# Half of the weighted one-hots of a route quad move from VectorE to ScalarE

## The chip, the cores and the metric

The kernel runs on one core of one Trainium2 chip. The time is the device time of one execution in microseconds; the median of several runs counts. A row of the trace gives a start on the clock of the one profiled execution, in microseconds from its first instruction.

## The reference, cut to what matters

Two layers of a streaming encoder. Each has a mixer of three attention branches, which the change does not touch, and then a PEER layer: for each of 512 tokens, product keys pick 16 of 128x128 experts for each of 8 heads, so 128 experts a token, each with a softmax share.

```python
def peer_ffn(h, w_q, sub_keys, u_tab, v_tab):
    ...
        q = (xb @ w_q).reshape(P_TOKEN_BLOCK, P_HEADS, 2, P_HALF)
        s = jnp.einsum('thcd,ckd->thck', q, sub_keys)
        sv, si = lax.top_k(s, P_TOPK)
        ...
        g = jax.nn.softmax(top_s, axis=-1).reshape(P_TOKEN_BLOCK, P_HEADS * P_TOPK)
        a = jax.nn.gelu(jnp.einsum('td,ted->te', xb, u), approximate=False) * g
        return jnp.einsum('te,ted->td', a, vv)
```

## The kernel before, in words

**Two ways through the expert layer.** The first 128 tokens go the sparse way: the rows of their experts are gathered, one gather for each of the 128 picks, and VectorE takes a dot product with each. The other 384 tokens (`DENSE`) go the dense way: TensorE multiplies them with all experts, 128 of them (a column) at a time, in 128 columns, and the result is weighted later with a route matrix that holds each token's share at the experts picked and zero elsewhere.

**The stages** of the expert layer are `query`, `select`, `route`, `rest` and `down`. The first four work through the columns; `down` multiplies with the second table. The change lies in `route`: 2 steps of 24 columns. Layer 0's first step begins at about 1351.5 in the trace, its second at 1523.3.

**A column** is one tile of 128x1024. SyncE loads it into one of four slots of `W`. ScalarE rounds it (`lead`, L1244 to L1250: `u_hi`), GpSimd subtracts (`lower`, L1417: `u_lo`), TensorE makes the product in three parts, 24 matmuls (`product`, L664 to L666), ScalarE reads it through gelu (`read_column`, L1264) and stores it with a DMA of its own queue (L1266). `u_hi` and `u_lo` have four buffers, the product two banks.

**The route matrix** is made beside it. For one token it is the product of two one-hot matrices over the 128 picks: where the first key index stands, and where the second stands, weighted with the share. Four tokens are a quad. VectorE makes the four plain one-hots in one instruction (L1862, `oh_i`) and the four weighted ones in four (L1865, `oh_g`: is_equal with the index, then times the share, both pointers into `pickT`), four quads in a ring. TensorE multiplies them (`quad`, L1026, 4 fp32 matmuls in 8 records) between the products of a column, and ScalarE copies the result out of its bank (`copy_routes`, L1304), three banks in turn. Eight quads fill a buffer of 2 MB, which goes out in one DMA (L1308).

`QUADS` places 48 quads a step in columns 0 to 21: two a column (behind the products of k=3 and k=7), three in columns 4, 9, 14 and 19 (k=2, 5, 7), so column c starts with quad 2c + c//5. Columns 22 and 23 have none.

**Sparse rows beside it.** Behind the one-hots of quad q, VectorE takes the dot product of the row 24+48*step+q (`sparse_up`, L1776). GpSimd issues the gathers (`gather`, L1425) into 8 slots, in a fixed order: four behind the subtraction of the first column of `route`, from row 24 on, and two behind the subtraction of each later column. Ahead of each it waits until the row 8 before has been used.

**Order on each engine in a column n of `route`.** ScalarE: `lead(n)`, the copies of the quads of column n-2, the gelu of column n-2. VectorE: quad by quad, held by its rows and by the quad four before. GpSimd: subtraction n, two gathers. Each is a queue that a late wait holds entirely.

**At the end of `select`** VectorE computes the picks and their shares; `copy_picks` copies them, transposed by TensorE (`turn_picks`), from PSUM into `pickT`, three times a layer.

Of the kernel before, what the change touches and what calls it, by code (L numbers as in the profile page):

```python
# [40 lines left out]
ALU = mybir.AluOpType  # L41
ACT = mybir.ActivationFunctionType
AX = mybir.AxisListType
ds = bass.ds
# [5 lines left out]
TT = T // 128  # L50
# [10 lines left out]
DENSE = T - SPARSE  # L61
# [13 lines left out]
COLUMNS = {"query": 6, "select": 12, "route": 24, "rest": 8}  # L75
# [137 lines left out]
def build_trunk(nc, x_t, stream, vecs, consts, c_t, gate_tiles, z_dram, tab_u, tab_v, u_rows, v_rows, out_t, route_dram, act_dram, layers=LAYERS):  # L213
# [3 lines left out]
    with ctx:  # L217
        def sb(name, shape, dt=F32):
            return ctx.enter_context(nc.sbuf_tensor(name, shape, dt))

        def sem(name):
            return ctx.enter_context(nc.semaphore(name))
# [3 lines left out]
        def signal(name, per_step, credit=8):  # L226
            signals.append(Signal(sem(name), per_step, credit))
            return signals[-1]
# [83 lines left out]
        route = [carve(128 * TOKENS, [128, TOKENS]) for _ in range(2)]  # L312
        cand = carve(HEADS * 256, [HEADS, 256])
        onehot16 = carve(HEADS * 256, [HEADS * 16, 16])
        pickT = carve(3 * DENSE, [3, DENSE])

        oh_i = cand.rearrange("p h (b i) -> p (h b) i", i=128).rearrange("p (b t) i -> p b t i", t=4)
        oh_g = onehot16.rearrange("p n c -> p (n c)").rearrange("p (b t i) -> p b t i", b=4, t=4)
# [18 lines left out]
        assert shared + 16 * DENSE <= shared + 2 * 128 * TOKENS + 2 * HEADS * 256  # L337
        sb("selection", [128, ARENA - shared - (4 * 2 + 8 + 8) * DENSE])
        gathered_rows = sb("gathered_rows", [128, 6, D])


        PS = [ctx.enter_context(nc.psum_tensor(f"bank{i}", [128, 512], F32)) for i in range(4)]
# [6 lines left out]
        def cst(name):  # L349
            a, w = CONST[name]  # L350
            return C[:, a:a + w]
# [22 lines left out]
        held = sem("held")  # L374
# [56 lines left out]
        picks_ready = signal("picks_ready", {"select": 3})  # L431
        picks_turned = signal("picks_turned", {"picked": 1})
        picks_copied = signal("picks_copied", {"picked": 1})

        Q = DENSE // 2 // 4
        QUADS = {}
        first = 0
        for n in range(COLUMNS["route"]):
            width = 0 if n >= 22 else 3 if n % 5 == 4 else 2
            QUADS[n] = list(range(first, first + width))  # L440
            first += width
        assert first == Q, first
        iota_placed = sem("iota_placed")
        onehots_i = signal("onehots_i", {"route": Q})
        onehots_g = signal("onehots_g", {"route": Q})
        route_product = signal("route_product", {"route": Q})
# [85 lines left out]
        def u_buffer(stage, n):  # L532
            return n % 4
# [124 lines left out]
        def _(pe):  # L658
# [227 lines left out]
            with pe.Fori(0, layers) as layer:  # L886
# [35 lines left out]
                if "gates" in stages:  # L922
                    enter(pe, "gates", layer)
                    with pe.Fori(0, 4) as step:
                        for g in range(6):
                            i = g % 3
# [4 lines left out]
                            last = project(PS[2 + g % 2][:], wb[:, (g % 2) * 512:(g % 2) * 512 + 512], oT[i], kts=4)  # L931
# [12 lines left out]
                if "experts" in stages:  # L944
# [76 lines left out]
                    def quad(step, q):  # L1021
                        pe.wait_ge(onehots_i.sem, onehots_i.at("route", layer, step, q + 1))
                        pe.wait_ge(onehots_g.sem, onehots_g.at("route", layer, step, q + 1))
                        pe.wait_ge(route_copied.sem, route_copied.at("route", layer, step, q - 2))
                        for t in range(4):
                            last = mm(PS[q % 3][:, t * 128:(t + 1) * 128], oh_i[:, q % 4, t, :], oh_g[:, q % 4, t, :],  # L1026
                                      start=True, stop=True)
                        last.then_inc(route_product.sem, 1)
# [34 lines left out]
                    for k in range(KT):  # L1063
                        last = nc.tensor.transpose(pair[:, k * 128:(k + 1) * 128],
                                                   gathered_rows[:, 0, k * 128:(k + 1) * 128], cst("ident"))
                    last.then_inc(sparse_turned, 1)
                    for i, bank in enumerate(DENSE_BANKS):
                        pe.wait_ge(y_copied, layer * 6 + (i + 1))
                        pe.sem_inc(held, 1)
                        for c in range(4):  # L1070
                            d0 = i % 2 * 512 + c * 128
                            last = nc.tensor.transpose(PS[bank][:, c * 128:(c + 1) * 128],
                                                       gathered_rows[:, 1 + i // 2, d0:d0 + 128], cst("ident"))
# [4 lines left out]
        def _(act):  # L1078
            chain = Chain(act, scalar_chain)
            fn = nc.scalar.activation  # L1080
# [114 lines left out]
            with act.Fori(0, layers) as layer:  # L1195
# [43 lines left out]
                if "experts" in stages:  # L1239
# [4 lines left out]
                    def lead(stage, step, n):  # L1244

                        raw, loaded, value = tile(stage, layer, step, n)
                        act.wait_ge(loaded, value)

                        act.wait_ge(col_done.sem, col_done.at(stage, layer, step, n - 3))
                        fn(u_parts[0][:, u_buffer(stage, n), :], raw, ACT.Copy).then_inc(col_hi.sem, 1)  # L1250
# [7 lines left out]
                    def read_column(stage, step, n):  # L1258

                        act.wait_ge(col_done.sem, col_done.at(stage, layer, step, n + 1))  # L1260

                        i = n - QUERY_TILES if stage == "query" else n
                        act.wait_ge(act_stored[n % 2].sem, act_stored[n % 2].at(stage, layer, step, 16 * (i // 2)))
                        fn(act_out[:, n % 2, :], PS[6 + n % 2][:, 0:DENSE], ACT.Gelu).then_inc(col_read.sem, 1)  # L1264
                        act.wait_ge(col_read.sem, col_read.at(stage, layer, step, n + 1))
                        act.dma_start(act_dram[:, ds(column(stage, step, n) * DENSE, DENSE)], act_out[:, n % 2, :]  # L1266
                                      ).then_inc(act_stored[n % 2].sem, 16)

                    def exponentials(step):
                        act.wait_ge(pick_shifted.sem, pick_shifted.at("select", layer, step, 1))  # L1270
                        t2 = top.rearrange("p h k -> p (h k)")
                        fn(t2, t2, ACT.Exp).then_inc(pick_exp.sem, 1)
# [22 lines left out]
                    def copy_routes(step, n):  # L1295

                        for q in QUADS[n]:
# [8 lines left out]
                            if q % 8 == 7:  # L1306
# [2 lines left out]
                                              route[b].rearrange("p j t -> p (j t)")  # L1309
                                              ).then_inc(route_stored[b].sem, 16)  # L1310

                    exponentials(TT - 1)
                    with act.Fori(0, STEPS["route"]) as step:
                        for n in range(COLUMNS["route"]):
                            lead("route", step, n)
                            if n >= 2:
                                copy_routes(step, n - 2)
                            read_column("route", step, n - 2)
                    for n in range(COLUMNS["rest"]):
                        lead("rest", 0, n)  # L1320
                        if n == 4:
                            act.wait_ge(row_used.sem, row_used.at("late", layer, 0, 8))
                            act.sem_inc(held, 1)
                            fn(dots, dots, ACT.Gelu).then_inc(sparse_gelu, 1)
                        read_column("rest", 0, n - 2)
# [134 lines left out]
        def _(dve):  # L1460
            chain = Chain(dve, vector_chain)
            chain.held = held
            stt, tt, ts = nc.vector.scalar_tensor_tensor, nc.vector.tensor_tensor, nc.vector.tensor_scalar
# [168 lines left out]
            with dve.Fori(0, layers) as layer:  # L1632
# [16 lines left out]
                for stage in ("swa_kv", "swa", "mla_c", "mla", "fox"):  # L1649
# [5 lines left out]
                    else:  # L1655
                        step = 0
# [27 lines left out]
                if "gates" in stages:  # L1684
                    enter(dve, "gates", layer)
                    with dve.Fori(0, 4) as step:
# [3 lines left out]
                        for g in range(6):  # L1690
                            e, i = g // 3, g % 3
# [25 lines left out]
                if "experts" in stages:  # L1717
# [44 lines left out]

                    def copy_picks(step):
                        dve.wait_ge(picks_turned.sem, picks_turned.at("picked", layer, step - 1, 1))
                        nc.vector.tensor_copy(pickT[:, :, ds((step - 1) * 128, 128)],
                                              PS[2][:, 0:384].rearrange("p (n t) -> p n t", n=3)
                                              ).then_inc(picks_copied.sem, 1)
# [81 lines left out]
                    for step in range(2):  # L1849
                        for q in range(Q):  # L1850
                            if step == 0 and q == 2:
                                copy_picks(TT - 1)
                                dve.wait_ge(picks_copied.sem, picks_copied.at("picked", layer, 2, 1))
                                dve.sem_inc(held, 1)
                            elif step == 0 and q == 0:
                                dve.wait_ge(picks_copied.sem, picks_copied.at("picked", layer, 1, 1))
                                dve.sem_inc(held, 1)

                            dve.wait_ge(route_product.sem, route_product.at("route", layer, step, q - 3))
                            four = step * (DENSE // 2) + 4 * q  # L1860
                            iota = PS[3][:, 0:128]
                            tt(oh_i[:, q % 4], pickT[:, 0, four:four + 4].unsqueeze(2).broadcast_to([128, 4, 128]),  # L1862
                               iota.unsqueeze(1).broadcast_to([128, 4, 128]), ALU.is_equal).then_inc(onehots_i.sem, 1)
                            for t in range(4):
                                last = ts(oh_g[:, q % 4, t, :], iota, pickT[:, 1, four + t:four + t + 1],  # L1865
                                          pickT[:, 2, four + t:four + t + 1], ALU.is_equal, ALU.mult)
                            last.then_inc(onehots_g.sem, 1)
                            sparse_up(24 + Q * step + q)
# [250 lines left out]
```

## Time and profile before

| what | value |
| --- | --- |
| time, median of 3 runs | 4606.48 us (4606.35 to 4607.62) |
| the profiled execution, its own time | 4604.27 us |
| its span, first to last instruction | 4602.2 us |
| TensorE busy | 4099.5 us, 89% |
| VectorE busy | 2647.3 us, 58% |
| ScalarE busy | 1511.9 us, 33% |
| GpSimd busy | 1265.6 us, 27% |
| DMA, mean over the span | 197 GB/s |
| mean granted TensorE clock | 0.951 |

The shares are averages over stages. In the rows below, PE is TensorE's matmuls, DVE VectorE, ACT ScalarE, POOL GpSimd. A time in brackets is idle time just before the instruction, and behind the arrow stands what ended it.

### The profile page before, as it was taken

What the parts mean: (1) busy time and instruction counts of PE and PEld (TensorE: products, weight loads), DVE (VectorE), ACT (ScalarE), POOL (GpSimd) and SP (SyncE); (2) the same over time, 40 slices, a digit from 0 to 9 for tenths busy, and PEclk for the clock granted to TensorE, in tenths of its full rate; (3) what the DMA queues carried; (4) which work ended last, traced back from release to release, by engine and by line L of the source; (5) the groups of instructions that cost most, each with busy time, mean ns of one, the idle gap of its engine ahead of it and who ended that gap; (6) DMA issues with size and microseconds to landing.
All of it is one profiled execution on the core that took longest, in us unless ns stands there. A gap on an engine that the chain in (4) does not pass through costs nothing.

```text
span 4602.2 us, 62131 instructions
## 1 busy us (share of the span) xinstructions
PE 4099.5 (89%) x18422; PEld 3032.7 (66%) x18422; DVE 2647.3 (58%) x5668; ACT 1511.9 (33%) x2426; POOL 1265.6 (27%) x884
## 2 busy tenths in 40 slices
PE   4987899989998989999859878999899989899998
PEld 1433356459998887777724334564699988877776
DVE  3433323236899867777735233222368998677776
ACT  2223323233443433333322233331334434333332
POOL 0000000025775662222100000000258756522221
PEclk8998999999999999999979989999999999999999
DMA  4430111324679889999634311113247789899996
GB/s 172 137 105 30 39 55 41 110 93 138 228 257 347 324 330 321 330 331 340 224 143 135 98 37 46 41 41 119 90 144 242 260 320 337 333 320 327 333 333 231
DMA packets 340821, 906.78 MB, mean 197 GB/s; under 512 B 28688, under 2 KB 160016, under 8 KB 337168
## 3 DMA queue, kind: packets, MB, share of 16 engines
q1 hardware_dynamic: 215824, 497.49, 32.3%
q0 software_dynamic: 84480, 306.22, 17.9%
q10 hardware_dynamic: 40320, 100.68, 5.7%
q8 instruction: 94, 1.54, 0.1%
q14 instruction: 103, 0.84, 0.1%
HBM read 788.94 MB, written 115.34 MB: 196 GB/s over the span
## 4 chain that ended last, share of the span: by engine, by line
PE 45%; issue 16%; DVE 15%; DMA 14%; POOL 4%; ACT 3%; DVEq 1%; POOLq 0%; ACTq 0%; SPq 0%; PEldq 0%
PE bank L675 12%; DMA W<-tab_v 12%; PE bank L740 7%; PE bank L664 4%; PE bank L666 4%; PE bank L665 4%; DVE u_lo L1906 3%; POOL gathered_rows L1425 2%; PE bank L767 2%; PE bank L800 2%; PE bank L726 2%; PE bank L718 1%; DVE arena L1816 1%; DVE gathered_rows L1776 1%; PE bank L710 1%
## 5 line engine op out<-in xcount | busy, mean ns | idle before, releaser
L1417 POOL TENSOR_TENSOR u_lo<-W,u_hi 128x1024 fp32r<-128x1024 f32 x272 | 688.6, 2533 | 1190.6 <-ACT u_hi L1250 1188.7
L664 PE MATMUL bank<-h_hi,u_hi 128*128 128x384 f32 (+1 forms) x2176 | 764.5, 351 | 50.6 <-POOL u_lo L1417 43.8
L666 PE MATMUL bank<-h_hi,u_lo 128*128 128x384 f32 (+1 forms) x2176 | 744.3, 342 | 0.0
L665 PE MATMUL bank<-h_lo,u_hi 128*128 128x384 f32 (+1 forms) x2176 | 744.2, 342 | 0.0
L664 PE MATMUL bank<-u_hi,a_hi 128*128 128x512 f32 x1536 | 606.8, 395 | 55.1 <-DVE a_lo L1910 47.0
L665 PE MATMUL bank<-u_lo,a_hi 128*128 128x512 f32 x1536 | 601.9, 392 | 0.0
L666 PE MATMUL bank<-u_hi,a_lo 128*128 128x512 f32 x1536 | 601.9, 392 | 0.0
L1333 ACT ACTIVATE u_hi<-W 128x1024 fp32r<-128x1024 f32 x256 | 272.5, 1065 | 724.4 <-PE bank L666 374.4
L664 PEld LDWEIGHTS bank<-h_hi,u_hi 128*128 128x128 f32 x2176 | 416.6, 191 | 61.0 <-issue 43.6
L665 PEld LDWEIGHTS bank<-h_lo,u_hi 128*128 128x128 f32 x2176 | 416.6, 191 | 5.4
L666 PEld LDWEIGHTS bank<-h_hi,u_lo 128*128 128x128 f32 x2176 | 415.2, 191 | 5.5
L1425 POOL DMA_INDIRECT gathered_rows<-v_rows,arena x192 | 206.4, 1075 | 645.8 <-DVE banks4and L1885 636.3
L664 PEld LDWEIGHTS bank<-u_hi,a_hi 128*128 128x128 f32 x1536 | 290.8, 189 | 134.7 <-issue 75.5
L740 PE MATMUL bank<-hT,gate_raw 128*128 128x512 f32 x768 | 375.1, 618 | 1.0 <-ACT mixT L1163 0.8
L1387 POOL DMA_DIRECT2D gate_raw<-gate_tiles x48 | 25.7, 535 | 1151.0 <-ACT mixT L1163 985.6
L1250 ACT ACTIVATE u_hi<-W 128x1024 fp32r<-128x1024 f32 x272 | 288.3, 1061 | 160.4 <-ACT act_out L1264 150.5
L666 PEld LDWEIGHTS bank<-u_hi,a_lo 128*128 128x128 f32 x1536 | 290.8, 189 | 61.3
L665 PEld LDWEIGHTS bank<-u_lo,a_hi 128*128 128x128 f32 x1536 | 291.1, 190 | 59.3
L675 PE MATMUL bank<-hT,W 128*128 128x512 f32 (+1 forms) x544 | 269.4, 654 | 54.7 <-POOLq L482 23.4
L1906 DVE TENSOR_TENSOR u_lo<-W,u_hi 128x1024 fp32r<-128x1024 f32 x256 | 311.7, 1217 | 4.9 <-ACT u_hi L1333 4.9
L1576 DVE TENSOR_REDUCE arena<-bank 128x1 f32<-128x128 f32 (+3 forms) x128 | 62.8, 491 | 434.1 <-PE bank L776 434.1
L1910 DVE TENSOR_TENSOR a_lo<-act_in,a_hi 128x384 fp32r<-128x384 f32 x256 | 142.5, 557 | 267.7 <-ACT a_hi L1339 267.6
(186 smaller groups left out, 6150.2 us busy)
## 6 DMA issues: line engine op xcount, KB each, us to landing
W<-tab_u SPq DMA_DIRECT2D x256, 512.0 KB, 3.9
W<-tab_v SPq DMA_DIRECT2D x256, 512.0 KB, 8.9
W<-stream SPq DMA_DIRECT2D x206, 512.0 KB, 3.7
act_scratch<-act_out ACTq DMA_DIRECT2D x256, 192.0 KB, 4.2
route_scratch<-arena ACTq DMA_DIRECT2D x24, 2048.0 KB, 10.2
act_in<-act_scratch SPq DMA_DIRECT2D x64, 768.0 KB, 5.8
g_cur<-route_scratch SPq DMA_DIRECT2D x64, 768.0 KB, 9.5
gate_raw<-gate_tiles POOLq DMA_DIRECT2D x48, 512.0 KB, 4.2
```

Of the source, the lines that this page charges most:

```text
L664: mm(out, w[0], a[0], start=first, stop=False)
L665: mm(out, w[0], a[1], start=False, stop=False)
L666: return mm(out, w[1], a[0], start=False, stop=last)
L675: last = mm(out, w[:, k * pitch + off:k * pitch + off + width], act[:, k, :], start=(k == 0), stop=(k == kts - 1))
L726: last = mm(bank[:, t * 128:(t + 1) * 128], act[:, src + k, t * 128:(t + 1) * 128], w[:, k * pitch + off:k * pitch + off + 128], start=(k ...
L740: last = mm(GATE_BANK[stage][:], gate_raw[:, i, k * 128:(k + 1) * 128], hT[:, k, :], start=(k == 0), stop=(k == KT - 1))
L1250: fn(u_parts[0][:, u_buffer(stage, n), :], raw, ACT.Copy).then_inc(col_hi.sem, 1)
L1333: fn(u_parts[0][:, j % 4, :], raw, ACT.Copy).then_inc(col_hi.sem, 1)
L1417: nc.gpsimd.tensor_tensor(u_parts[1][:, b, :], raw, u_parts[0][:, b, :].bitcast(F32), ALU.subtract).then_inc(col_lo.sem, 1)
L1425: nc.gpsimd.indirect_dma_start(gather_slot(k), None, u_rows if k < SPARSE else v_rows, bass.IndirectOffsetOnAxis(ap=row[:, k % SPARSE:k % ...
L1906: tt(u_parts[1][:, j % 4, :], raw, u_parts[0][:, j % 4, :].bitcast(F32), ALU.subtract).then_inc(v_lo_done.sem, 1)
L1910: tt(a_parts[1][:, j % 4, :], a, a_parts[0][:, j % 4, :].bitcast(F32), ALU.subtract).then_inc(a_lo_done.sem, 1)
```

## The change

ScalarE makes the weighted one-hots of tokens 2 and 3 of a quad, in the first two quads of each column (`HALVED`, 44 of 48 quads), in place. It takes the absolute distance between the position and the index, and then a rectifier: relu(share - share * distance) is the share where the distance is 0, and zero where it is 1 or more. For that it needs the shares with the sign turned (`minus_share`), which VectorE writes in `copy_picks`. VectorE makes tokens 0 and 1, and all four in a third quad. ScalarE does this behind the gelu of column n-2 for the quads of column n. TensorE's quad waits for one more semaphore.

```diff
+        minus_share = sb("minus_share", [128, DENSE])
...
+        HALVED = [quads[i] for quads in QUADS.values() for i in range(len(quads)) if i < 2]
+        distances = signal("distances", {"route": 2 * len(HALVED)})
+        onehots_a = signal("onehots_a", {"route": len(HALVED)})
...
                         pe.wait_ge(onehots_g.sem, onehots_g.at("route", layer, step, q + 1))
+                        if q in HALVED:
+                            pe.wait_ge(onehots_a.sem, onehots_a.at("route", layer, step, HALVED.index(q) + 1))
...
+                    def weighted_onehots(step, q):
+
+                        nth = HALVED.index(q)
+                        act.wait_ge(route_product.sem, route_product.at("route", layer, step, q - 3))
+                        four = step * (DENSE // 2) + 4 * q
+                        for t in range(2, 4):
+                            fn(oh_g[:, q % 4, t, :], cst("iota"), ACT.Abs, bias=pickT[:, 1, ds(four + t, 1)], scale=-1.0
+                               ).then_inc(distances.sem, 1)
+                        for t in range(2, 4):
+                            act.wait_ge(distances.sem, distances.at("route", layer, step, 2 * nth + t - 1))
+                            last = fn(oh_g[:, q % 4, t, :], oh_g[:, q % 4, t, :], ACT.Relu,
+                                      bias=pickT[:, 2, ds(four + t, 1)], scale=minus_share[:, ds(four + t, 1)])
+                        last.then_inc(onehots_a.sem, 1)
...
                         for n in range(COLUMNS["route"]):
+                            if n == COLUMNS["route"] - 2:
+                                act.wait_ge(picks_copied.sem, picks_copied.at("picked", layer, 2, 1))
+                                act.sem_inc(held, 1)
                             lead("route", step, n)
                             if n >= 2:
                                 copy_routes(step, n - 2)
                             read_column("route", step, n - 2)
+                            if n == 0:
+                                act.wait_ge(picks_ready.sem, picks_ready.at("select", layer, TT - 1, 3))
+                                act.sem_inc(held, 1)
+                            for q in QUADS[n][:2]:
+                                weighted_onehots(step, q)
...
                         dve.wait_ge(picks_turned.sem, picks_turned.at("picked", layer, step - 1, 1))
+                        ts(minus_share[:, ds((step - 1) * 128, 128)], PS[2][:, 256:384], -1.0, None, ALU.mult)
...
-                            for t in range(4):
+                            for t in range(2 if q in HALVED else 4):
                                 last = ts(oh_g[:, q % 4, t, :], iota, pickT[:, 1, four + t:four + t + 1],
```

## Rows read from the trace of the kernel before

**Rows 1.** The page's busy time (share of the span) and instructions of each engine.

```profile
PE 4099.5 (89%) x18422; PEld 3032.7 (66%) x18422; DVE 2647.3 (58%) x5668; ACT 1511.9 (33%) x2426; POOL 1265.6 (27%) x884
```

**Rows 2.** Windows of the first route step, layer 0, in three parts.

```profile
core 0: us, PE busy (x) PEld busy (x) DVE busy (x) ACT busy (x) POOL busy (x), PEclk, DMA share, GB/s
1351.50:1411.00 59.50, 59.21 (x379) 58.10 (x378) 59.27 (x140) 23.50 (x37) 39.47 (x28) 0.96 0.88 329
1411.00:1478.40 67.40, 62.35 (x408) 59.07 (x408) 64.66 (x150) 26.44 (x40) 41.41 (x29) 1.00 0.92 344
1478.40:1523.30 44.90, 30.68 (x179) 29.21 (x177) 29.26 (x70) 13.79 (x20) 16.57 (x13) 0.89 0.65 244
```

**Rows 3.** Timeline of VectorE: start, us, instruction, from one quad to the next.

```profile
1455.34 0.68 DVE L1862 TENSOR_TENSOR arena<-arena,bank 128x512 f32<-128x512 f32 x1
1455.94 1.36 DVE L1865 TENSOR_SCALAR arena<-bank,arena 128x128 f32<-128x128 f32 x4
...
1458.35 0.68 DVE L1862 TENSOR_TENSOR arena<-arena,bank 128x512 f32<-128x512 f32 x1
```

**Rows 4.** Timeline of TensorE, column 15 with two quads, up to column 16.

```profile
1452.25 0.42 PE L664 MATMUL bank<-h_hi,u_hi 128*128 128x384 f32 x1
...
1453.38 0.33 PE L664 MATMUL bank<-h_hi,u_hi 128*128 128x384 f32 x1
...
1453.90 0.33 PE L664 MATMUL bank<-h_hi,u_hi 128*128 128x384 f32 x1
...
1454.43 1.08 PE L1026 MATMUL bank<-arena 128*128 128x128 f32 x8
...
1458.28 0.42 PE L664 MATMUL bank<-h_hi,u_hi 128*128 128x384 f32 x1
```

**Rows 5.** Timeline of TensorE, the two longest waits for a quad.

```profile
1491.48 2.05 PE L1026 MATMUL bank<-arena 128*128 128x128 f32 x8 [5.84 <-issue]
...
1508.54 1.13 PE L1026 MATMUL bank<-arena 128*128 128x128 f32 x8 [2.52 <-issue]
```

**Rows 6.** Timeline of ScalarE and GpSimd behind the start of column 15.

```profile
1452.61 0.60 ACT L1304 ACTIVATE arena<-bank 128x512 f32<-128x512 f32 x1 [2.49 <-PE bank L1026]
...
1453.11 0.49 ACT L1264 ACTIVATE act_out<-bank 128x384 f32<-128x384 f32 x1
...
1454.26 1.06 ACT L1250 ACTIVATE u_hi<-W 128x1024 fp32r<-128x1024 f32 x1 [0.67 <-ACT act_out L1264]
...
1455.40 2.40 POOL L1417 TENSOR_TENSOR u_lo<-W,u_hi 128x1024 fp32r<-128x1024 f32 x1 [4.56 <-ACT u_hi L1250]
...
1457.95 0.94 POOL L1425 DMA_INDIRECT gathered_rows<-u_rows,arena  x1 [0.15 <-issue]
```

**Rows 7.** Timeline of VectorE, its waits for rows 66 and 70.

```profile
1488.27 1.22 DVE L1776 SCALAR_TENSOR_TENSOR gathered_rows<-gathered_rows,banks4and 128x1024 f32<-128x1024 f32 x1 [4.91 <-DMA gathered_rows<-u_rows,arena]
...
1505.33 1.22 DVE L1776 SCALAR_TENSOR_TENSOR gathered_rows<-gathered_rows,banks4and 128x1024 f32<-128x1024 f32 x1 [4.91 <-DMA gathered_rows<-u_rows,arena]
```

**Rows 8.** Gathers: medians to landing, 1440 to 1480; row 66's issue; all of L1425.

```profile
gathered_rows<-u_rows,arena POOLq DMA_INDIRECT x8, 6.7
W<-u_rows,arena POOLq DMA_INDIRECT x4, 5.8
...
1477.91 0.94 POOL L1425 DMA_INDIRECT gathered_rows<-u_rows,arena  x1
...
DMA to landing us min/median/max: 4.3/7.2/12.3
```

**Rows 9.** Groups of ScalarE by form: busy, mean ns, then idle before.

```profile
L1272 ACT ACTIVATE arena<-arena 128x128 f32<-128x128 f32 x4 | 1.2, 310 | 0.0
...
L1123 ACT ACTIVATE arena<-arena 128x512 f32<-128x512 f32 x30 | 18.9, 629 | 0.3
...
L1096 ACT ACTIVATE hT<-hT,modT 128x512 f32<-128x512 f32 x32 | 21.4, 722 | 3.3 <-DVE hT L1490 3.3
...
L1264 ACT ACT_TABLE_LOAD x12 | 15.4, 1283 | 8.4 <-PE bank L666 8.3
```

**Rows 10.** Timeline of TensorE, the last transposes of the picks.

```profile
1350.99 0.90 PE L985 MATMUL bank<-C,arena 128*128 128x128 f32 x3 [7.23 <-DVE arena L1834]
```

## The prediction

> **What bounds the kernel now.** I read the page's busy shares first: ScalarE is busy a third of the span [rows 1], so it looks free to take work. An average hides stages, so I then cut the route stage, the only one in which the changed lines run, with the windows view. The reader is to see three parts in a step of 24 columns [rows 2]: 59.5 us in which TensorE hardly idles, 67.4 us in which it idles 5.0, and 44.9 us in which it is busy 30.7 and DMA moves only 244 GB/s. This pattern comes four times (two steps in each of two layers). What bounds it has two parts.
>
> The first is VectorE's pace. It does one quad (four one-hots by index, four weighted ones, one dot product) each 3.02 us [rows 3]. TensorE needs 6.03 us for a column with two quads; its 24 products take 4.17 of them (0.52 for three), so a quad is 0.93 [rows 4]. Five columns with 11 quads take it 31.1 us and VectorE 33.2. VectorE starts ahead, and when TensorE has caught it, short waits come: the 5.0 us of idle of the second part. By the sum of the columns the loss up to 1478.4 is more, 7.2 us: 126.9 passed, and 19 columns and 41 quads need 117.3, the cold start 2.4 (0.04 of the clock missing over 59.5 us). These waits are what the change removes.
>
> The second is a loop that these small waits hide. The timeline from column 15's start (1452.25) shows it [rows 4, 6]: ScalarE's gelu, then its rounding of the tile of column 17 at 1454.26, then GpSimd's subtraction at 1455.40, and behind that in GpSimd's order the gathers of two rows, the first at 1457.95. So the gathers tied to column m leave 5.7 us and more after TensorE begins column m-2. Counting them, they are rows 26+2m and 27+2m, while quad q+1 is built behind the dot product of row 24+q. Quads come at 2.2 a column and rows at 2, so the lead runs out towards a step's end. The model must predict where: quad 43 (the third of column 19, row 66) and quad 47 (row 70). There VectorE waits 4.91 us each time for exactly these rows [rows 7], and the same pair of waits stands at the same counts in the next step and in both of layer 1; TensorE then waits 5.84 and 2.52 [rows 5]. Waits of the dot product are of DMA, not of freed buffers. From a landed row to the quad on TensorE are 3.2 us (1488.27 to 1491.48) [rows 5, 7]. A landing takes 6.7 us in the median of 1440 to 1480; row 66 left at 1477.91 and took 10.4 [rows 7, 8]. The loop is thus 5.7+6.7+3.2 = 15.6 us over two columns, 2.2 of them in the column itself before its first quad: (15.6-2.2)/2 = 6.7 us a column where it binds (columns 15 to 18), against 6.54 measured (1452.25 to 1478.4, four columns). The two limits lie on each other there.
>
> **The change, part by part.** *VectorE* loses two of four weighted one-hots in 44 of 48 quads: each is 0.32 us (1.28 for four) [rows 3], so 0.64 a quad, which is 2.38 instead of 3.02, or 26.8 us per five columns, below TensorE's 31.1. Its pace stops binding. The third quads of columns 4, 9, 14 and 19 keep all four.
>
> *ScalarE* gains four activations of 128x128 a quad, eight a column in columns 0 to 21. No row shows one with a bias by pointer at this size. From below: 310 ns, the exponential without one. The pointer's price is 722-629 = 93 ns at 128x512 [rows 9]. So Abs is 403 ns and Relu, with two pointers, 496. Activations in a row start 0.1 before the last ends (copy 0.60 long, gelu 0.50 behind it [rows 6]), and the first Relu's wait for the first Abs is covered by the second Abs: 2x0.30+2x0.40 = 1.4 us a quad, W = 2.8 a column. With no pointer price it is 2.4 from the rows' lower end, and with 0.1 for each semaphore and register address it is 3.6. I take 2.8, since the semaphore waits ahead of gelu in the rows cost nothing visible.
>
> By the Trainium skill, ScalarE: Activation LUTs, "What ACT_TABLE_LOAD costs", a pointer adds about 93 ns and neighbours overlap by as much; its figures give 387 and 479 ns and 2.7 us a column, and the sum below would be some 2 us smaller. The same page's "Rules for kernel authors" puts relu on VectorE and not ScalarE, which speaks against this change; the rows agree in that two one-hots cost 0.64 us there and 1.4 here.
>
> Where they stand matters more. They come behind the gelu of column n-2 and ahead of the next `lead`. Queued behind them are that rounding, GpSimd's subtraction, its two gathers, and the route copies. The subtraction has cover: it ends at S+5.5 now and is needed at S+12. The copies free banks needed two quads later. The gathers have none: the loop grows by 2.8 and loses 0.6 (VectorE's shorter one-hots, not for quad 43). ScalarE's own column: 2.7 us from second copy to the end of the rounding, 0.6 for the other copy, 2.8 new: 6.1 of TensorE's 6.03, and 31.0 of 31.1 in five columns. Full, but just fitting.
>
> *The sum for one step*, against measured starts of columns. Columns 0 to 14: TensorE alone takes 93.2 us (15 columns of 4.17, 33 quads) and the cold start 2.4, so 95.6; the longer loop, 17.8, asks 6.3 a column from 10 to 14 at the second quad (5.2 into the column), +0.4. 96.0 against 100.75 now: -4.75. Columns 15 to 18: (17.8-2.2)/2 = 7.8 each, 31.2 against 26.15: +5.05. Column 19's third quad: 5.7+2.8+10.4+3.2 = 22.1 after column 18's start, 14.3 after column 19's, against 13.1: +1.2. Quad 47: +2.8-0.6 = +2.2. Columns 22 and 23 have no quads, and the next step starts with its lead restored. Sum +3.7 a step, +14.8 for four.
>
> *VectorE's scaled copy* (`minus_share`, 128x128 from PSUM, 0.4 us as one of L1865: 1.36 less three of 0.32 [rows 3]) comes three times a layer. Two lie in `select` ahead of the last reduction, for which TensorE waits 7.23 us [rows 10]: 0.8 a layer, +1.6. The third has cover at the route's start. ScalarE's new wait for the picks holds its second rounding until TensorE turns them at 1350.99: 2.8 us of activations, 1.1 of rounding and 2.4 of subtraction end at 1357.3, and TensorE's first column, begun at 1351.5, lasts 6.03 at the least. I cost it at nothing; without that cover it would be a microsecond or two a layer.
>
> Together +16.4. The profiled execution took 4604.3 in all, 4602.2 of it span; the median is 4606.5, 2.2 above. I add to the median: 4622.9.
>
> The bounds of the landing time: at 6.0 us (TensorE slower, so DMA less loaded) a step costs +1.8, at 7.2 +6.0. Total +9 to +26.
>
> **Rivals.** *Slower by the gathers' loop* (forecast), 4612 to 4640: chance 0.50. For it: the late rows fall where the count puts them, in both steps. Against: the landing time may fall as the demand on DMA does.
>
> *Faster: rows land early enough.* If landings fall to 4.9 us, between the shortest of all (4.3) and the 5.8 of the gathers into tile slots [rows 8], and row 66's to 8, the loop is 16.0 and columns 15 to 18 take 6.9: -4.75-0.4+1.45 = -3.7, then -0.3 and +0.6, -3.4 a step, -12 in all with the copies: 4594.5. It decides below a landing of about 5.7. Had the loop no weight at all, all 7.2 us of small waits a step would go: about 4578. For it: these waits are real and VectorE's. Against: DMA is at 344 GB/s in that part [rows 2]. Chance 0.17.
>
> *No change*: at landings near 5.7 gain and loss cancel, 4606. Chance 0.17, with small results of the forecast's case.
>
> *ScalarE becomes the bound*: at W = 3.2 its column is 6.5, five take 33, as slow as VectorE before; then nothing is won in columns 0 to 14 (+0.65), 15 to 18 go at 8.0 (+5.85), and the late quads cost +1.4 and +2.6: +10.5 a step, 4650. At 3.6 it is +18 a step, 4680. It decides at W above 2.9. Chance 0.14.
>
> *Table loads*: if Abs does not share a table with gelu, two loads of 1283 ns [rows 9] come in each column: 8.7 us for ScalarE, 2.1 a column above today for 88 columns, about 4790. Copies among gelus cost no such load now (12 loads for 256 gelus, at stage and loop heads). Chance 0.02. The Trainium skill, ScalarE: Activation LUTs, "Table sets: the hidden batching unit", says that relu, copy and abs are in every set; by that rule this case is out, and no run here shows Abs yet.
>
> **How the numbers follow.** Time: the likeliest case, 4623. Within 0.2% (9 us) is what a measurement of this kernel can tell from none. Slower: 0.50 less a tenth of it that ends within 9 us, plus 0.14 and 0.02, rounded to 0.62; same 0.21; faster 0.17. The range takes the early-landing case from 4592 and ScalarE's case up to 4655. The forecast's own range is 4612 to 4640.
>
> **What would show it.** In the profile after: the dot product's waits for DMA grow and begin before 1480; gathers leave about 8.5 us after the start of column m-2, no longer 5.7; the dot products of VectorE start 2.4 us apart where no row is late; TensorE's waits of 0.3 to 0.8 us in 1411 to 1450 (the second part) are gone; eight new activations a column last 0.4 and 0.5 us and no table load stands among them; columns 15 to 18 last 7.8 us. Wrong it would be if the rows are waited for no longer than before, if W is not near 2.8, or if the landing time falls with the load.

## The result

The changed kernel takes 4677.4 us (median of 4 runs), the kernel before 4607.1 beside it. One of the four runs of the kernel before took 5535 us and is left out of the ratio. The ratio is 1.0162, 95% interval 1.0146 to 1.0178. The kernel is slower by 70 us by the medians and by 75 by the ratio. The forecast was slower, 4623, with 4655 as the upper end of the range. The direction was right and the size, 16.4 us, was too small by a factor of more than four.

The page of the changed kernel gives its busy times, to be read against [rows 1]:

```profile
PE 4122.2 (88%) x18422; PEld 3063.8 (66%) x18422; DVE 2536.0 (54%) x5322; ACT 1737.9 (37%) x3130; POOL 1263.5 (27%) x884
```

VectorE lost 111 us of work, ScalarE gained 226, and TensorE, whose program is the same, is busy 23 us longer. Longer for the same matmuls means a lower clock. The windows view of the first route step of layer 0 shows where (columns as in [rows 2]; the step begins 3.4 us later here, and its parts are cut at the same distances, the last one at the step's end):

```profile
core 0: us, PE busy (x) PEld busy (x) DVE busy (x) ACT busy (x) POOL busy (x), PEclk, DMA share, GB/s
1354.90:1414.40 59.50, 58.00 (x383) 57.71 (x383) 50.12 (x107) 50.98 (x119) 39.88 (x28) 0.98 0.87 316
1414.40:1481.80 67.40, 52.88 (x312) 51.72 (x311) 41.30 (x87) 41.90 (x96) 36.83 (x27) 0.86 0.79 299
1481.80:1545.20 63.40, 48.68 (x273) 47.50 (x271) 32.84 (x70) 29.57 (x59) 23.91 (x18) 0.87 0.64 234
```

The step takes 190.3 us against 171.8. TensorE's idle time is 30.7 us of it (190.3 less 159.6 busy) against 19.5, so +11.2, and its busy time is 159.6 against 152.3, so +7.3. The forecast's sum was +3.7. The middle part, where nothing but short waits stood before, is now idle for 14.5 us at a mean clock of 0.86, where it had been 1.00.

What ScalarE does is as costed. Its timeline behind a gelu (as [rows 6]):

```profile
1451.32 0.48 ACT L1270 ACTIVATE act_out<-bank 128x384 f32<-128x384 f32 x1
...
1452.47 0.69 ACT L1324 ACTIVATE arena<-C,arena 128x128 f32<-128x128 f32 x2 [0.66 <-ACT act_out L1270]
1453.07 0.87 ACT L1328 ACTIVATE arena<-arena,minus_share 128x128 f32<-128x128 f32 x2
1453.84 0.68 ACT L1324 ACTIVATE arena<-C,arena 128x128 f32<-128x128 f32 x2
1454.43 0.86 ACT L1328 ACTIVATE arena<-arena,minus_share 128x128 f32<-128x128 f32 x2
1455.19 1.05 ACT L1256 ACTIVATE u_hi<-W 128x1024 fp32r<-128x1024 f32 x1
```

W is 2.72 us (1452.47 to 1455.19), forecast 2.8. Now GpSimd, behind a column that TensorE began at 1450.44:

```profile
1456.32 2.38 POOL L1445 TENSOR_TENSOR u_lo<-W,u_hi 128x1024 fp32r<-128x1024 f32 x1 [6.02 <-ACT u_hi L1256]
1458.86 0.95 POOL L1453 DMA_INDIRECT W<-u_rows,arena  x1 [0.16 <-issue]
```

The gathers leave 8.4 us behind that start, forecast 8.5, where it was 5.7 (over the four steps the median is 8.9, and 5.7 before). Up to here the costs held. What did not is what follows a late row. VectorE's two longest waits for a row in the middle part, and TensorE's waits that hang on them:

```profile
1420.47 1.22 DVE L1805 SCALAR_TENSOR_TENSOR gathered_rows<-gathered_rows,banks4and 128x1024 f32<-128x1024 f32 x1 [7.34 <-DMA gathered_rows<-u_rows,arena]
1445.93 1.22 DVE L1805 SCALAR_TENSOR_TENSOR gathered_rows<-gathered_rows,banks4and 128x1024 f32<-128x1024 f32 x1 [10.47 <-DMA gathered_rows<-u_rows,arena]
```

```profile
1423.68 2.05 PE L1032 MATMUL bank<-arena 128*128 128x128 f32 x8 [5.07 <-issue]
...
1448.74 2.05 PE L1032 MATMUL bank<-arena 128*128 128x128 f32 x8 [4.33 <-DVE arena L1894]
```

By count these are rows 44 and 50. The reader is to see the length of the quad behind each wait: 2.05 us, where a quad at full clock is 1.05 to 1.13. The windows around the first stall:

```profile
1414.40:1423.60 9.20, 4.21 (x30) 3.89 (x28) 3.13 (x8) 4.73 (x11) 7.13 (x6) 0.94 0.99 386
1423.60:1430.00 6.40, 6.32 (x26) 6.35 (x27) 6.40 (x14) 3.57 (x10) 0.00 (x0) 0.55 0.67 256
```

TensorE idles 5.0 us, and in the 6.4 us after it the granted clock is 0.55, nearly all of it at the lower level of 1.2 GHz. By my estimate that costs 2.9 us more (0.45 of 6.4). In this step five waits of 4.25 to 5.07 us have such a quad of 2.05 us behind them; before there was one (5.84 us) for a quad [rows 5], and one for a column at the step's end.

Why rows 44 and 50? The timeline of issues around the second:

```profile
1433.80 0.94 POOL L1453 DMA_INDIRECT gathered_rows<-u_rows,arena  x1 [0.15 <-issue]
...
1434.22 0.34 ACTq L1314 DMA_DIRECT2D route_scratch<-arena  x1
```

The row leaves 0.4 us ahead of a store of 2 MB and lands 12.1 us after its issue (1445.93 less 1433.80). In this step VectorE waits more than 4 us for rows 36, 44, 50, 58, 64, 66 and 70. Rows 36, 44, 50, 58 and 66 left within 2 us of a store (1381.8, 1407.0, 1434.2, 1464.8, 1497.4) and took 9.1 to 12.1 us; all others that were waited for took 4.9 to 7.8, rows 64 and 70 among them, which left late because a stall had held ScalarE. In the kernel before, rows 50 and 58 left 1.5 and 1.6 us ahead of their store (1423.54 and 1448.65, stores at 1425.0 and 1450.3) and landed in 5.6 and 4.9 us. The delay has moved them beside and behind it.

The room of a row shrank from both sides. Row 36 had 12.3 us between its issue and its use before, and has 6.0 now. Counted from the step's start it leaves 2.4 us later, and VectorE, which has less to do for each quad, wants it 3.9 us earlier.

### The profile page after: what moved, and what is told of

The parts are those of the page before. It is cut to its first block, busy times and chain, and to the rows that moved or that the text cites. A ratio compares the mean times of both kernels' runs of the same rounds, so it can differ in the third digit from the quotient of the medians.

```text
span 4674.2 us, 63919 instructions
## 1 busy us (share of the span) xinstructions
PE 4122.2 (88%) x18422; PEld 3063.8 (66%) x18422; DVE 2536.0 (54%) x5322; ACT 1737.9 (37%) x3130; POOL 1263.5 (27%) x884
## 4 chain that ended last, share of the span: by engine, by line
PE 45%; issue 16%; DMA 15%; DVE 14%; POOL 3%; ACT 3%; DVEq 1%; POOLq 0%; SPq 0%; ACTq 0%; PEldq 0%
PE bank L679 12%; DMA W<-tab_v 12%; PE bank L744 7%; PE bank L668 4%; PE bank L670 4%; PE bank L669 4%; DVE u_lo L1935 3%; POOL gathered_rows L1453 2%; PE bank L771 2%; PE bank L804 2%; PE bank L730 2%; PE bank L722 1%; DMA gathered_rows<-u_rows,arena 1%; DVE arena L1845 1%; DVE gathered_rows L1805 1%
## 5 line engine op out<-in xcount | busy, mean ns | idle before, releaser
L1805 DVE SCALAR_TENSOR_TENSOR gathered_rows<-gathered_rows,banks4and 128x1024 f32<-128x1024 f32 x192 | 230.8, 1214 | 239.9 <-DMA gathered_rows<-u_rows,arena 239.6
L1032 PE MATMUL bank<-arena 128*128 128x128 f32 x1536 | 223.2, 292 | 110.8 <-DVE arena L1894 71.0
```

Source lines behind the costliest of these rows:

```text
L1805: stt(gather_slot(k), gather_slot(k), 1.0, pair[:], ALU.mult, ALU.mult, accum_out=dots[:, k:k + 1]).then_inc(row_used.sem, 1)
```

## The experiments

Ratios are to the kernel before, from runs beside it on the same chip; the level of both drifts by a few tenths of a per cent from chip to chip, so only ratios are compared.

### The rounding first (e1_lead_first)

```diff
                             lead("route", step, n)
...
+                            if n >= 1:
+                                for q in QUADS[n - 1][:2]:
+                                    weighted_onehots(step, q)
                             if n >= 2:
                                 copy_routes(step, n - 2)
                             read_column("route", step, n - 2)
...
-                            for q in QUADS[n][:2]:
-                                weighted_onehots(step, q)
```

The wait for the picks (not shown) moves with it, to n = 1. All work stays where it is but for the rounding, which ScalarE now does ahead of it.

> Theory A (the order on ScalarE is the cost: the activations stand ahead of the rounding on which GpSimd's gathers hang): with the rounding first the gathers leave 5.7 us after the start of column m-2 as before, VectorE keeps its 2.38 us a quad, and the time falls from 4677 below 4607, to 4580 to 4605. Rival B (the work itself is too much for ScalarE, 6.1 us of a 6.03 us column): it stays at 4650 or above.

Measured: 4614.5 us, ratio 1.0006 (0.9992 to 1.002). The whole loss is gone. ScalarE does the same 352 pairs of activations, so its load is not what costs; Rival B falls. The copies and the gelu still stand behind the activations here, so their delay does not cost either. In the trace of e1 the gathers leave 6.1 us (median of the four steps) after TensorE begins column m-2, against 8.9 in the changed kernel. But the time does not fall below the kernel before, as theory A had it: the upper end of the expectation was 4605.

### VectorE's relief alone (e3_vector_relief)

```diff
-                            for t in range(4):
+                            for t in range(2 if q % 11 in (0, 1, 2, 3, 4, 5, 6, 7, 8, 9) else 4):
```

(In the kernel before; in 44 of 48 quads two weighted one-hots are simply left out.)

> The kernel before with two of the four weighted one-hots left out in 44 of 48 quads and nothing added on ScalarE, so the output lacks their part. Theory A: the short waits of TensorE for VectorE go, up to 7.2 us a step, 4578 to 4595. Rival (the gathers' loop takes all of it back): 4600 to 4607.

Measured: ratio 1.0004 (0.9993 to 1.0015). The rival is right: VectorE's 0.64 us a quad buy nothing at all, with nothing put on ScalarE. The waits view of this kernel for its first step (engine, line, what it waited for, us, times, longest):

```profile
DVE gathered_rows L1776 <- DMA gathered_rows<-u_rows,arena: 36.9, 10, 6.1
PE bank L1026 <- issue: 10.6, 5, 6.8
...
PE bank L1026 <- DVE arena L1862: 5.3, 2, 3.8
```

and the same view of the kernel before:

```profile
PE bank L1026 <- issue: 14.3, 13, 5.8
DVE gathered_rows L1776 <- DMA gathered_rows<-u_rows,arena: 12.5, 5, 4.9
```

VectorE gains time and spends it waiting for rows: 44 us with the tile slots' 7.4, against 12.5. TensorE's waits for quads are no shorter in sum, 15.9 us against 14.3, but they are 7 and not 13. By columns: 0 to 14 take 100.1 us against 100.7, of a credit of 4.75, and 15 to 18 take 30.4 against 26.1. The window of the step:

```profile
1350.90:1525.80 174.90, 153.37 (x962) 151.02 (x961) 123.79 (x262) 63.34 (x96) 97.46 (x68) 0.93 0.82 308
```

The granted clock of the step is 0.93, and 0.96 before. TensorE is busy for 153.4 us in it, against 152.3: the lower clock is a small part of the price, 1.1 us.

### VectorE's old pace in the changed kernel (e2_vector_pace_kept)

```diff
                             last.then_inc(onehots_g.sem, 1)
+                            if q in HALVED:
+                                for t, out in ((2, vec("keys")), (3, PS[3][:, 128:256])):
+                                    last = ts(out, iota, pickT[:, 1, four + t:four + t + 1],
+                                              pickT[:, 2, four + t:four + t + 1], ALU.is_equal, ALU.mult)
...
```

(Not shown: a semaphore by which VectorE waits for its own earlier writes of these two.)

> The changed kernel, but VectorE also writes two further weighted one-hots that nobody reads in each of the 44 quads, so that its quad takes 3.02 us again. Theory A: the loop of the gathers grows by 0.6 us and VectorE's old pace comes back in columns 0 to 14, 4685 to 4720. Rival (VectorE's relief bought nothing in the changed kernel): 4677 within 5.

Measured: ratio 1.011 (1.0087 to 1.0133), no slower than the changed kernel and a little faster. My 4685 to 4720 is a miss, and so is the rival's 4677 within 5, both on the side that e3 shows: VectorE's work is not the bound in either kernel. The relief even costs something here: without it the ratio is 1.011, with it 1.0162. That fits row 36, which VectorE wants earlier for it, but the two intervals are only 0.13% apart and were not measured side by side, so it is not settled.

### Rows gathered early (e4_gathers_ahead and e6_before_gathers_ahead)

```diff
-                            for _ in range(4 if c == 0 else 2):
+                            for _ in range(4 if c == 0 else 3 if c in (3, 6) else 2):
```

The same line in the changed kernel (e4) and in the kernel before (e6). From column 6 of the first step on, each row leaves one column earlier. The buffers were free long before.

> The changed kernel with two more rows gathered early, one each behind the subtraction of columns 3 and 6 of the first step, so that from there each row leaves a column earlier. Theory A (late rows are what costs): most of the 70 us come back, 4600 to 4625. Rival B (ScalarE is too full): 4665 to 4677, since nothing on ScalarE changes.

> The kernel before with only the two rows gathered early. Theory A: late rows go and VectorE's pace of 3.02 us a quad, 145 us for 48 quads, is the bound, 4560 to 4580; so the move to ScalarE is worth 15 to 40 us once rows leave early. Rival (the gathers were the whole gain and VectorE's work is worth nothing even then): 4540 to 4550.

Measured: e4 0.986 (0.9835 to 0.9885), e6 0.9862 (0.9844 to 0.988). Two gathers moved in each layer turn 75 us lost into 65 gained, with ScalarE's program as it was in the changed kernel. My 4600 to 4625 for e4 was too careful by 50 us. And the kernel before gains as much: the rival of e6 is right, and the move to ScalarE is worth nothing even here. TensorE's waits of e6 in the middle part:

```profile
1443.52 1.13 PE L1026 MATMUL bank<-arena 128*128 128x128 f32 x8 [0.30 <-issue]
1446.54 1.13 PE L1026 MATMUL bank<-arena 128*128 128x128 f32 x8 [0.29 <-issue]
1449.55 1.13 PE L1026 MATMUL bank<-arena 128*128 128x128 f32 x8 [0.84 <-issue]
...
1476.69 1.13 PE L1026 MATMUL bank<-arena 128*128 128x128 f32 x8 [0.30 <-issue]
```

Only the short ones are left, and they repeat after 33.2 us (1443.5 to 1476.7), VectorE's five columns. So in columns 0 to 14 of this step e6 runs at VectorE's pace (99.6 us, three times 33.2); columns 15 to 18 take 24.1, TensorE's own 6.03 each. Its granted clock is 0.97 in the step, and the step takes 159.0 us. e4, with VectorE relieved, takes 157.5: columns 0 to 14 take 94.9, so that the credit of the forecast is there once the rows leave early, but columns 15 to 18 take 27.8, and VectorE waits 29.8 us for rows again.

### Both mends, and more lead (e5_lead_first_gathers_ahead, e8_further_ahead)

e5 has the edits of e1 and e4. e8 has the third gather in columns 3, 5, 7 and 9.

> Both mends of the changed kernel: the rounding ahead of the activations, and two more rows gathered early. Theory A: with a 15.0 us loop and a column more of lead only the rows behind a store of 2 MB are late, 4530 to 4545. Rival (the order on ScalarE no longer matters once rows leave early): 4545 to 4550, as the gathers alone gave.

> The rounding first and four rows gathered early, in columns 3, 5, 7 and 9, so that rows leave two columns ahead. Theory A: the rows behind a store are in time too and TensorE's own 290 us a layer with DMA's rate are the bound, 4515 to 4530. Rival (the eight slots are full and GpSimd waits for them ahead of a subtraction): 4540 or more.

Measured: e5 0.9885 (0.9867 to 0.9902), e8 0.9848 (0.9827 to 0.987). Once the rows leave early, the order on ScalarE does not matter; e5's rival holds. e8 took 4538.3 us, between its theory (4515 to 4530) and its rival (4540 or more). It has the lowest ratio of all, but its interval overlaps those of e4 and e6.

### The store in pieces (e7_store_in_pieces, e9_all_three, e10_before_ahead_pieces)

```diff
-                                act.dma_start(route_dram[:, ds(step * 6 + group, 1), :].rearrange("p a n -> p (a n)"),
-                                              route[b].rearrange("p j t -> p (j t)")
-                                              ).then_inc(route_stored[b].sem, 16)
+                                for piece in range(4 if q == Q - 1 else 1):
+                                    store_piece(step, group, piece)
+                            elif q % 8 in (1, 3, 5) and group > 0:
+                                store_piece(step, group - 1, (q % 8 + 1) // 2)
```

`store_piece` stores 32 of the 128 partitions, 512 KB; the waits count four pieces. e7 is the changed kernel with it, e9 is e5 with it, e10 is e6 with it.

> The changed kernel with each 2 MB store of the route matrix cut into four of 32 partitions, issued two quads apart; same bytes. Theory A with the store as the cause of the late eighth rows (landings of 10 to 12 us against 5 to 7): those landings fall below 9 and the time to 4625 to 4655. Rival (gathers are late from the bytes of a whole column, however placed): 4670 to 4680.

> Rounding first, two rows gathered early, and the route store in four pieces. Theory A with DMA's bytes as the next bound: the same as with two of the three, 4535 to 4550. Rival (the store's burst is what still delays rows): 4515 to 4530.

> The kernel before with two rows gathered early and the store in four pieces, VectorE's one-hots as they were. If VectorE's pace is now the bound: 4535 to 4545, no better than without the pieces. Rival (the burst of the store is): 4515 to 4530.

Measured: e7 1.0103 (1.0072 to 1.0133), e9 0.9858 (0.9835 to 0.9882), e10 0.988 (0.9854 to 0.9905). In the changed kernel the pieces give back some 27 us of the 75 (1.0162 less 1.0103), which ends at the upper end of theory A's range. The waits of e7 in its first step:

```profile
DVE gathered_rows L1813 <- DMA gathered_rows<-u_rows,arena: 40.3, 22, 8.7
```

22 waits where the changed kernel has 9, of 44.9 us in sum: the lateness is spread more than it is gone. Rows that left between 1 us ahead of a piece and 4 us behind it landed in 5.4 to 13.5 us, 7.6 in the median. Beside a whole store of the changed kernel they took 9.1 to 13.6 us, 10.5 in the median. The mean clock of the whole kernel is 0.950, against 0.944 in the changed kernel.

The 27 us are a balance, for the pieces have a price of their own. The last group's four are issued in a row, which holds ScalarE's queue at the step's end (e7, then the changed kernel):

```profile
1516.59 4.96 ACTq L1304 DMA_DIRECT2D route_scratch<-arena  x4
```

```profile
1532.32 0.34 ACTq L1314 DMA_DIRECT2D route_scratch<-arena  x1
```

Columns 22 and 23 of the four steps together take 64.8 us in e7 and 46.7 in the changed kernel. Columns 0 to 21 take 660.9, against 706.2 in the changed kernel and 632.3 before: in them the pieces give 45 of 74 us back. With the rows early, e9 and e10 show no gain in sum; there too the last two columns take 2 to 6 us a step longer (18.4 to 20.9 in the first step of a layer, against 13.4 to 15.9 in e5, e6 and e8).

### Half of the delay (e11_one_of_four)

```diff
-                        for t in range(2, 4):
+                        for t in range(3, 4):
...
-                        for t in range(2, 4):
...
+                        for t in range(3, 4):
...
-                            for t in range(2 if q in HALVED else 4):
+                            for t in range(3 if q in HALVED else 4):
```

> The changed kernel with one of four weighted one-hots on ScalarE (token 3) and three on VectorE, in the same place: W is half, 1.4 us a column. Theory A (the delay of the rounding is the cost, about in proportion): 4630 to 4650. Rival (it costs only once ScalarE's column is as long as TensorE's): 4600 to 4615.

Measured: 1.0119 (1.009 to 1.0147), about 55 us, more than the 4630 to 4650 expected. Theory A holds against its rival, for ScalarE is far from full here, but "in proportion" is wrong: half of W gives three quarters of the loss, within wide intervals.

### Late rows and nothing else (e12_before_gathers_behind)

```diff
-                            for _ in range(4 if c == 0 else 2):
+                            for _ in range(2):
```

(In the kernel before: neither ScalarE's nor VectorE's work is touched, and each row leaves a column later.)

> The kernel before with two instead of four gathers behind the first subtraction, so that each row leaves a column later, and nothing else. Theory A (late rows alone slow the route, whatever delays them): more than the 70 us of the changed kernel, whose rows leave 2.8 us later; 4700 to 4800. Rival (the delay is not what costs; ScalarE's work is): 4607 to 4640.

Measured: 4853.4 us, ratio 1.0493 (1.0464 to 1.0523), above the 4700 to 4800 expected. Its first step takes 227.0 us at a clock of 0.85:

```profile
1352.90:1579.90 227.00, 167.07 (x963) 163.21 (x961) 147.75 (x341) 63.41 (x96) 93.32 (x67) 0.85 0.62 230
```

That is +55.2 for the step, with 59.9 us of it idle, for rows one column (at least 6 us) later. Late rows alone slow the route, with nothing changed on ScalarE or VectorE.

## Why the prediction was wrong

*Right, and measured.* The place: the work stands ahead of the rounding, behind which the gathers hang (e1 gives all of the loss back; e12 makes a larger one without ScalarE). W, 2.72 us for 2.8; Abs 391 ns for 403, Relu 480 for 496. The gathers' departure, 8.4 us for 8.5. VectorE's quad, 2.38 us (1452.57 to 1454.94 in the trace after). No table load stands among the new activations:

```profile
L1328 ACT ACTIVATE arena<-arena,minus_share 128x128 f32<-128x128 f32 x352 | 152.8, 480 | 0.7 <-ACT arena L1324 0.6
L1324 ACT ACTIVATE arena<-C,arena 128x128 f32<-128x128 f32 x352 | 121.4, 391 | 86.5 <-ACT act_out L1270 49.6 <-DVE arena L1863 17.5 <-PE bank L1032 14.4
...
L1270 ACT ACT_TABLE_LOAD x12 | 15.4, 1283 | 8.4 <-PE bank L670 8.3
```

The loads are the 12 of before [rows 9]. The trace agrees with the Trainium skill, ScalarE: Activation LUTs, in both places where it was drawn on: abs and relu share gelu's table ("Table sets: the hidden batching unit"), and its durations (387 and 479 ns, 2.7 us a column) are nearer than mine.

*The step that failed* is the sum for one step, in its term for columns 0 to 14 and in the landing time behind it. The first step, by columns:

| columns | before, us | forecast | measured |
| --- | --- | --- | --- |
| 0 to 14 | 100.7 | -4.75 | +8.9 |
| 15 to 18 | 26.1 | +5.05 | +6.0 |
| 19 to 21 | 31.1 | +3.4 | +3.4 |
| 22 and 23 | 13.8 | 0 | +0.2 |

Columns 15 to 18 last 8.0 us each, forecast 7.8. Over the four steps columns 0 to 14 cost 26 us where the forecast gained 19, and columns 19 to 21 cost 23 where it had 14. So three quarters of the miss lie where the forecast saw a gain.

The sum took a landing of 6.7 us, a median, for every row but 66, and so expected no delay in columns 0 to 9 and 0.4 us in columns 10 to 14. But rows issued beside a store of the route matrix, from about 1 us ahead of it to 4 us behind it, take 9 us and more. I saw it for row 66 and did not ask which rows share its place. Before, their room covered most of them: row 44 took 11.3 us and had 11.4. The later departure and the earlier use uncover them, from row 36 on. A median says nothing of a loop that stops for its slowest member.

*A term that was missing:* TensorE's clock falls behind a long stall. Behind the five long waits of the first step it was granted 0.50 to 0.53 for 3.3 to 5.9 us. The sum counted the clock at the step's start and nowhere else. In the first step it is the +7.3 us of busy time beside +11.2 of idle, two fifths of the loss. By the Trainium skill, TensorE: Matmul & The Clock Gate, "HAM oscillation — how this bites in real kernels", a DMA wait that returns in each round of a loop is paid twice, once as idle and once as slow matmuls behind it; the rows after agree, with 0.55 over 6.4 us behind a wait of 5.07.

*A credit that was wrong:* the 4.75 us for VectorE's short waits in columns 0 to 14. e3 gives that credit alone and gets nothing: with VectorE faster, TensorE reaches the late rows sooner and waits there instead. That the small waits were real did not make them a gain. They become one only with the rows early (columns 0 to 14 of e4 against e6, 4.6 us). What stands behind e3 in detail (which row hides behind which wait) is read from its trace, not tried by itself.

*A small term that was not there:* the 1.6 us for `minus_share` in `select`. From a layer's first gather to the start of `route` are 161.6 us in both kernels and both layers (1189.95 to 1351.54 and 1193.39 to 1354.98 in layer 0).

*Of the rivals,* ScalarE as the bound gave the nearest number, 4650 to 4680, and was false: e1 has the same load and no loss. The gathers' loop, the forecast, was the mechanism, with a price four times too small. "Rows land early enough" did not come: the median landing of the rows of the first table fell only from 6.9 to 6.6 us over the whole kernel, and the longest rose from 12.3 to 13.6. My reason, that a burst of 2 MB is as large at a lower mean rate, is not tried.

*Open.* Why half of W gives three quarters of the loss. And what the last microseconds hang on in e4, e5, e8 and e9, which all end at 0.985 to 0.989 as e6 does. Most of it is TensorE itself: in the steps of these five it is busy for 146 to 150 us and idle for 3 to 13; in a layer's first step some 5 of these lie at its end, where TensorE waits for the next step's first column. For the rest e6 goes at VectorE's pace in part, and e4 has rows late again, with DMA at a share of 0.92 in its first step:

```profile
1353.00:1510.50 157.50, 147.12 (x963) 145.33 (x961) 127.39 (x268) 121.45 (x273) 102.78 (x73) 0.98 0.92 349
```

No run here parts the two.

**The better kernel.** e6 is the kernel before with one line changed, 1.4% faster than it (0.9862) and 3% faster than the changed one; e8 does no worse with ScalarE's help. The line is worth having; for the move no gain is measured.

## What to carry to other kernels

Before work is put on an engine that is a third busy, ask what its queue issues next and who waits for that: two thirds idle time is of no use ahead of the one instruction that starts a loop through other engines. Give rows that are gathered from HBM a lead counted from the slowest landing beside the largest store, and look at whether buffers stand free: here the cure was two gathers issued earlier into slots that were free. Count a repeated long stall of TensorE at more than its idle time, and before crediting short waits ask what stands behind them: here late rows took the credit back.

## What the runs showed of the hardware that was not expected

A gather of 128 rows of 4 KB issued within 2 us of a 2 MB store took 9.1 to 12.1 us to be usable, and 4.9 to 7.8 us otherwise (the rows waited for in the changed kernel's first step), though the two are on different queues. Over all four steps of that kernel, 40 gathers issued between 1 us ahead of a store and 4 us behind it landed in 9.1 to 13.6 us, those 4 to 10 us behind in 5.9 to 9.6, and those more than 2 us ahead in 4.8 to 7.8. Waits of TensorE up to 1.1 us left the granted clock at 1.00 in the stretch from 1411 to 1478 of the kernel before; the five waits of 4.25 to 5.07 us in the changed kernel's first step were each followed by a quad of 2.05 us, twice its usual length. The length of the wait alone does not decide when the clock falls: in the second step one of 2.60 us was followed by a quad of 2.04 us, and one of 4.45 us by a quad of 1.27 and a granted clock of 0.53 only after that (1638.1 to 1641.2). In the kernel before, a wait of 2.52 us was followed by a quad of 1.13 [rows 5].

Four pieces of 512 KB issued in a row held ScalarE's queue for 4.96 us (e7), where one store of 2 MB took 0.34.
